# The kv, query and gate products of a sparse-attention layer: fp32 products against three split fp32r products

## The reference, cut to what matters

```python
def rmsnorm(x, g):
    return x * rsqrt(mean(x * x, -1) + EPS) * g

u  = rmsnorm(h, kv_norm)              # D = 1024
kv = (u @ kv_w)                       # 1024 x 1536: k_c v_c | k_s v_s k_w v_w (4 groups x 64 each)
k_s, k_w = rope(rmsnorm(k_s, ..)), rope(rmsnorm(k_w, ..))
k_cmp, v_cmp = compress(k_c, ..), compress(v_c, ..)   # 15 blocks of 32 tokens, two small matmuls, gelu
z  = rmsnorm(h, b_norm) @ b_w_in      # 1024 x (1024 queries + 48 gates)
q  = rope(rmsnorm(z[:, :1024]))       # 16 heads x 64
gates = sigmoid(z[:, 1024:] + gate_b)
o  = gates_0 * attend(q, k_cmp, v_cmp) + gates_1 * attend(q, k_s, v_s) + gates_2 * attend(q, k_w, v_w)
h  = h + o @ b_w_out
```

## Time and profile before

| | |
|---|---|
| median of 3 runs | 2376.24 us (2375.14 to 2376.44) |
| profiled execution | 2374.76 us, of which span 2373.1 us |
| busy in the span | PE 97%, DVE 72%, ACT 58%, POOL 4% |
| granted TensorE clock | mean 0.993 of full speed |
| end of ffn0 to the first `scores` | 297.43 to 408.27 us |
| attention steps | 408.27 to about 478 us |

### The profile page before, as it was taken

One profiled execution on the slowest core, in us unless ns is written; L12 is line 12 of the kernel. 1 busy time (PEld: TensorE's weight loads), 2 busy tenths in 40 slices (PEclk: granted clock), 3 DMA queues, 4 the chain that ended last, 5 costly groups with the idle time before them and its releaser, 6 DMA issues.

```text
span 2373.1 us, 31549 instructions
## 1 busy us (share of the span) xinstructions
PE 2307.4 (97%) x12242; PEld 1936.0 (82%) x12242; DVE 1698.0 (72%) x1609; ACT 1373.7 (58%) x1217; POOL 100.4 (4%) x111
## 2 busy tenths in 40 slices
PE   7999999999999999999999989999999999999998
PEld 6878845888889878888899788888888888888886
DVE  6655544755457676555567769898989888888897
ACT  4633312644336865334467557777777777777775
POOL 0000020000000110000011001000000000000020
PEclk9999999999999999999999999999999999999999
DMA  6455354055435335554353389999999999999993
GB/s 231 168 211 212 142 213 164 1 185 195 167 136 178 107 133 195 205 212 180 113 178 107 108 316 414 395 381 377 390 368 384 374 390 369 389 370 389 369 382 125
DMA packets 204633, 588.63 MB, mean 248 GB/s; under 512 B 9164, under 2 KB 17552, under 8 KB 204544
## 3 DMA queue, kind: packets, MB, share of 16 engines
q1 hardware_dynamic: 197696, 564.28, 63.8%
q0 software_dynamic: 6656, 23.04, 2.6%
q10 hardware_dynamic: 192, 0.05, 0.0%
HBM read 573.19 MB, written 14.16 MB: 247 GB/s over the span
## 4 chain that ended last, share of the span: by engine, by line
PE 94%; DVE 3%; ACT 1%; issue 1%; DMA 1%; ACTq 0%; DVEq 0%
PE ps L1386 9%; PE ps L1385 9%; PE ps L1387 9%; PE ps L781 8%; PE ps L783 8%; PE ps L782 8%; PE ps L666 4%; PE ps L1425 4%; PE ps L1424 4%; PE ps L1426 4%; PE ps L676 3%; PE ps L675 3%; PE ps L677 3%; PE ps L658 2%; PE ps L1159 1%; PE ps L1160 1%
## 5 line engine op out<-in xcount | busy, mean ns | idle before, releaser
L2038 DVE TENSOR_TENSOR more_low<-more_parts,high_parts 128x2048 fp32r<-128x2048 f32 x192 | 431.9, 2287 | 35.8 <-ACT high_parts L1494 34.7
L1494 ACT ACTIVATE high_parts<-more_parts 128x2048 fp32r<-128x2048 f32 x192 | 364.4, 1918 | 101.4 <-PE ps L1426 51.8
L1385 PE MATMUL ps<-high_parts,xmh 128*128 128x512 f32 x896 | 352.5, 393 | 2.4 <-issue 2.4
L1387 PE MATMUL ps<-high_parts,xml 128*128 128x512 f32 x896 | 349.1, 390 | 0.0
L2038 DVE TENSOR_TENSOR raw_low<-raw,high_parts 128x2048 fp32r<-128x2048 f32 x144 | 323.9, 2286 | 27.9 <-ACT high_parts L1494 27.9
L1494 ACT ACTIVATE high_parts<-raw 128x2048 fp32r<-128x2048 f32 x144 | 275.8, 1920 | 93.1 <-PE ps L1387 49.8
L1609 ACT ACTIVATE wh<-raw 128x4096 fp32r<-128x4096 f32 (+1 forms) x57 | 196.6, 3451 | 190.6 <-PE ps L783 179.8
L2209 DVE TENSOR_TENSOR wl<-raw,wh 128x4096 fp32r<-128x4096 f32 (+1 forms) x57 | 239.2, 4197 | 60.5 <-ACT wh L1609 60.5
L781 PE MATMUL ps<-wh,xh 128*128 128x512 f32 (+1 forms) x632 | 244.0, 386 | 3.4 <-issue 2.8
L783 PE MATMUL ps<-wh,xl 128*128 128x512 f32 (+1 forms) x632 | 239.6, 379 | 0.0
L782 PE MATMUL ps<-wl,xh 128*128 128x512 f32 (+1 forms) x632 | 239.5, 379 | 0.0
(11 more groups left out here) (545 smaller groups left out, 4441.7 us busy)
## 6 DMA issues: line engine op xcount, KB each, us to landing
more_parts<-in_moe_w_gate SPq DMA_DIRECT2D x78, 1024.0 KB, 5.1
more_parts<-in_moe_w_up SPq DMA_DIRECT2D x66, 1024.0 KB, 7.0
raw<-in_moe_w_down SPq DMA_DIRECT2D x64, 1024.0 KB, 6.4
more_parts<-in_moe_w_down SPq DMA_DIRECT2D x48, 1024.0 KB, 5.7
raw<-in_moe_w_up SPq DMA_DIRECT2D x46, 1024.0 KB, 5.3
raw<-in_w_in SPq DMA_DIRECT2D x22, 2048.0 KB, 8.0
raw<-in_f_w_in SPq DMA_DIRECT2D x20, 2048.0 KB, 8.6
raw<-in_moe_w_gate SPq DMA_DIRECT2D x34, 1024.0 KB, 6.8
```

Of the source, the lines that this page charges most:

```text
L1385: mm(o, xmh[:, k, :], hi[:, cs], start=(k == 0), stop=False)
L1387: t = mm(o, xml[:, k, :], hi[:, cs], start=False, stop=(k == KD - 1))
L1494: fn(part_high(j), part_raw(j), ACT.Copy).then_inc(hi_done, 1)
L2038: v.tensor_tensor(part_low(j), part_raw(j), part_high(j).bitcast(F32), ALU.subtract).then_inc(lo_done, 1)
```

## The change

The plain fp32 products of kv, queries and gates become split products. `uh` holds the high part of the transposed hidden state and `ul` the low part, without a norm weight. The norm weight goes into the weight tile: ACT writes high halves (`high_k`: weight times gain, as fp32r) and DVE low halves (`low_k`: weight times gain minus high). A half is 4 of the 8 steps `k` of one weight tile, 128 x 2048 elements; the list `K_HALVES` has eleven, with the buffer of the high part of each (`bh`, `wmh[:, 0]`, `wmh[:, 1]`, once `wmo[:, 0]`), and `k_free` says when a buffer's former reader is done.

```diff
+        K_HALVES = [(("kv", 0), "kv_norm", range(0, 4), 512, bh), (("kv", 0), "kv_norm", range(4, 8), 512, wmh[:, 1]),
+                    (("b_in", 0), "b_norm", range(0, 4), 512, wmh[:, 0]), (("b_in", 0), "b_norm", range(4, 8), 512, bh),
+                    (("b_in", 1), "b_norm", range(0, 4), 512, wmh[:, 1]), (("b_in", 1), "b_norm", range(4, 8), 512, wmh[:, 0]),
+                    (("b_in", 2), "b_norm", range(0, 8), 3 * NH, bh),
+                    (("kv", 1), "kv_norm", range(0, 4), 512, wmh[:, 1]), (("kv", 1), "kv_norm", range(4, 8), 512, wmh[:, 0]),
+                    (("kv", 2), "kv_norm", range(0, 4), 512, bh), (("kv", 2), "kv_norm", range(4, 8), 512, wmo[:, 0])]
# PE
+            def k_product(b, i, m, c0=0, n=None):
...
+                for k in ks:
+                    o, cs = ps[:, b, 0:n], slice(c0, c0 + n)
+                    mm(o, uh[:, k, ms], hi[:, k - ks[0], cs], start=(k == 0), stop=False)
+                    mm(o, uh[:, k, ms], lo[:, k, cs], start=False, stop=False)
+                    t = mm(o, ul[:, k, ms], hi[:, k - ks[0], cs], start=False, stop=(k == KD - 1))
...
+            queries_of(0)
+            queries_of(1)
 
             pe.wait_ge(kvc_in, 16 * 2 * 2 * NG)
...
-            product(me.a, ("b_in", 1), 1, ubT)
...
+            halves_split()
             for m in range(M):
-                product(me.v, ("b_in", 2), m, ubT, w=3 * NH)
+                k_product(me.v.claim(pe), 6, m).then_inc(v_filled, 1)
...
+            halves_split(2)
+            window_part(me.v, 0, 0)
             me.see(kc_ready)
...
+            window_part(me.a, 1, 0)
...
+            turn_keys(0)
+            window_part(me.v, 0, 256)
             turn_keys(1)
+            window_part(me.a, 1, 256)
+            released(("kv", 2), me.a)
# ACT
+            def high_k(i):
...
+                for k in ks:
+                    t = fn(hi[:, k - ks[0], :], src[:, k, :], ACT.Copy, scale=col(gain, k))
+                t.then_inc(mh_ready, 1)
# DVE
+            def low_k(i):
...
+                for k in ks:
+                    t = v.scalar_tensor_tensor(dst[:, k, :], src[:, k, :], col(gain, k), hi[:, k - ks[0], :].bitcast(F32),
+                                               ALU.mult, ALU.subtract)
+                t.then_inc(ml_ready, 1)
...
+            low_k(7)
+            low_k(8)
+            low_k(9)
+            low_k(10)
             keys_values(1)
# POOL
             po.wait_ge(zeroed_set, 1)
+            po.wait_ge(exp_done, 2)
```

More of the change, by code:

```diff
@@ L976, in _ @@
             turned_hidden = me.a.n
-            product(me.a, ("kv", 1), 1, uT)
-            released(("kv", 1), me.a)
+            halves_split(2)
+            b = me.v.claim(pe)
+            k_product(b, 7, 0)
+            k_product(b, 8, 0).then_inc(v_filled, 1)
             pe.wait_ge(a_read, turned_hidden)
@@ L1670, in ffn @@
                 body(nb - 1, FB, FB, last=True)
+                if ahead:
+                    ahead()
                 high_h_last(FFN_END[name] - 1)
-            ffn(0)
+            def high_k(i):
+                key, gain, ks, w, _ = K_HALVES[i]
+                arrived(act, key)
+                hi, src = k_high(i), tile_view(key, KD, w)
+                for k in ks:
+                    t = fn(hi[:, k - ks[0], :], src[:, k, :], ACT.Copy, scale=col(gain, k))
+                t.then_inc(mh_ready, 1)
+            ffn(0, ahead=lambda: high_k(0))
+            act.wait_ge(u_done, FFN_END["ffn0"])
+            high_k(1)
+            for m in range(M):
+                for j in range(2):
+                    b = me.s.take(act)
+                    fn(uh[:, 4 * j:4 * j + 4, m * P:(m + 1) * P], ps[:, b, :].rearrange("p (k t) -> p k t", k=4),
+                       ACT.Copy).then_inc(norm_h, 1)
+                squares(m)
+            square_root()
+            high_k(2)
             fn(ident_r[:], C("ident"), ACT.Copy).then_inc(causal_ready, 1)
             fn(causal_r[:], C("neg_causal"), ACT.Copy).then_inc(causal_ready, 1)
[L1678 to L1686, removed]
+            act.wait_ge(*k_free[0])
+            high_k(3)
             def root(n, rows=P):
@@ L1717, in _ @@
             root(NH // 2)
+            root(NH // 2)
+            act.wait_ge(*k_free[5])
+            high_k(7)
+            high_k(8)
             me.see(gate_ready)
@@ L1736, in _ @@
             t.then_inc(a_read, 1)
+            act.wait_ge(*k_free[6])
+            high_k(9)
+            high_k(10)
             root(NG)
+            root(NG, NCMP)
             keys_values(1)
             root(NG)
-            root(NG, NCMP)
+            root(NG)
+            b = me.a.take(act)
+            fn(kvn[:, 1, 768:1024], ps[:, b, 0:256], ACT.Copy, scale=small[:, 7:8]).then_inc(a_read, 1)
+            marks["keys", 2] = me.a.n
+            root(NG)
             turned_keys(0)
-            root(NG)
-            keys_values(2)
-            root(NG)
             turned_keys(1)
@@ L1747, in _ @@
             fn(cs[:], cs[:], ACT.Exp, scale=SCALE).then_inc(cexp_ready, 1)
+            b = me.a.take(act)
+            fn(vv[:, 1, 1, :, 0:HD], ps[:, b, 0:256].rearrange("p (g d) -> p g d", g=NG), ACT.Copy,
+               scale=small[:, 7:8]).then_inc(a_read, 1)
             def probs(i):
@@ L2294, in ffn, with low_turned @@
                 dve.nop().then_inc(d_added, 1)
[L2296 to L2306, removed]
+            def low_k(i):
+                key, gain, ks, w, _ = K_HALVES[i]
+                me.see(mh_ready)
+                hi, src, dst = k_high(i), tile_view(key, KD, w), tile_view(key, KD, w, raw_low)
+                for k in ks:
+                    t = v.scalar_tensor_tensor(dst[:, k, :], src[:, k, :], col(gain, k), hi[:, k - ks[0], :].bitcast(F32),
+                                               ALU.mult, ALU.subtract)
+                t.then_inc(ml_ready, 1)
+            def low_turned():
+                for j in range(2):
+                    b = me.s.take(dve)
+                    me.see(norm_h)
+                    ks, ms = slice(4 * j, 4 * j + 4), slice(me.low_m * P, (me.low_m + 1) * P)
+                    v.tensor_tensor(ul[:, ks, ms], ps[:, b, :].rearrange("p (k t) -> p k t", k=4), uh[:, ks, ms].bitcast(F32),
+                                    ALU.subtract).then_inc(s_read, 1)
+                me.low_m += 1
+            me.low_m = 0
+            ffn(0, beside=low_turned, ahead=lambda: low_k(0))
+            low_k(1)
+            low_turned()
             mean_squares()
+            low_k(2)
             b = me.v.take(dve)
@@ L2408, in _ @@
             t.then_inc(v_read, 1)
-            keys_values(2)
-            key_phase(1, 0)
+            key_phase(0, 1)
+            dve.nop().then_inc(k_ready, 1)
+            b = me.v.take(dve)
+            v.tensor_scalar(kvn[:, 0, 768:1024], ps[:, b, 0:256], small[:, 6:7], None, ALU.mult).then_inc(v_read, 1)
+            dve.wait_ge(v_read, me.v.n)
             b = me.v.take(dve)
```

97 lines of the change are left out of this document (66 added, 31 removed).

## The result

| | before | after |
|---|---|---|
| median | 2376.19 us (2375.02 to 2376.44, 8 runs) | 2383.80 us (2381.95 to 2384.74, 8 runs) |
| ratio to before | | 1.0030, 95% interval 1.0021 to 1.0040 |
| span of the profiled execution | 2373.1 us | 2382.7 us |
| granted TensorE clock, mean | 0.993 | 0.985 |

The page of after stands against the earlier trace rows: PE has no less busy time, but 4.3 us more (0.4 in after_again), although ten fp32 products have become split ones, and less of the last chain is PE's.

The account below looks back on a forecast made before the run. PE, busy 97% of the span, was taken as the bound. Scores 4.3 us earlier plus 1.1 from the clock, say 5.5, gave 2374.76 - 5.5 = 2369.3, plus 1.5 to the median's scale: 2370.7 us; range 2364 to 2380.

Parts of the forecast that it names:

- The step that failed: PE behind the xcT wait: transposes and gates until 346.0, then the compress product in 14.0 us, ending at 360.0.
- a gain of 1.1 at the scores: PE before the attention: last window parts, keys and scores at full rate, so the scores' 2.9 us shrink by 1.1.
- the forecast of the stage (5.4 less): Stage up to the attention: scores start 4.3 us earlier and run 1.1 us shorter, sum 5.4, say 5.5.
- the clock stays low: Rival, chance 0.10: half rate from the wait before 384 holds until the scores; gain about 1, so 2375 us.
- Split steps: PE's split products: three matmuls of 512 columns take 0.68 us, so eight k take 5.45 us instead of 6.9.
- Halves: Making weight halves: a high one 2.1 us on ACT, a low one 2.5 us on DVE, upper bound 3.0.
- Loads of kv: Weight loads for the compress product: kv 1 lands 8.5 us after release, kv 2 from 360.0 to 367.8.
- the weights come late: Rival, chance 0.16: kv 2 lands in 16.0 us instead of 7.8, a loss of 5.5, so 2381.7 us.
- Zeros in the attention: The write of zeros moves from 325 us into the attention, where queues are idle; cost 0.
- PE's 14.4 us less to do: PE's own work in the stage could shrink by 14.4 us; not taken as the gain, since halves must be made.
- The rule against it: Stage's head: POOL's fill of zeroed and DVE's low halves with two SBUF inputs contend, one waiting for the other.
- that rival (0.18): DVE held by the fill, chance 0.18: DVE waits 3.6 us, gain 2.4 to 0, about 2374.5 us.

Follow-up runs that it names:

- after_again: The changed kernel, unchanged, measured a second time: 2381.17 us, ratio 1.0016 to before.
- a7: Changed kernel with 48 gate matmuls dealt out among 24 wide ones, xc transposes behind them, gates and xcT ahead of the last two query norms on DVE: 2368.88 us.
- a5: Changed kernel with the low steps of kv 2 done a second time on DVE into a scratch tile: 2389.6 us, ratio 1.0057.
- b3: Kernel before with only the write of zeros moved to wait for the attention's second exp: 2376.11 us, ratio 0.9997.
- b2: Kernel before with the zeros' write late and DVE's xcT additions ahead of the last query norm: 2369.6 us, ratio 0.9973.
- a1: Changed kernel with 24 wide matmuls, result unused, on PE in its wait for xcT: 2377.86 us, ratio 1.0004.
- a2: Changed kernel with the gates' product ahead of the xc transposes on PE and the gate operations ahead of the xcT additions on DVE: 2372.21 us, ratio 0.9982.
- a4: Changed kernel with b_in 1 multiplied by tokens, xc transposes ahead of its last half, xcT ahead of the norms: 2372.64 us, ratio 0.9986.
- b1: Kernel before with DVE's xcT additions ahead of the last query norm: 2376.4 us, ratio 0.9995.
- a9: a4 with only high x high in the gates, 16 narrow matmuls instead of 48: 2370.63 us, ratio 0.9972.

## Why the prediction was wrong

Times of after are set back by 2.3 us here, by which its stage started later than before's.

**The step that failed** is the sentence "Four transposes and 48 gate matmuls, the first 20 or so at half rate, take it to 346.0; the compress product starts there ... and takes 14.0". I took the length of the half clock from before, 5 us after PE went on the earlier trace rows. But there a wide fp32 product followed the wait; the change had moved the gates to that place. All 48 ran at half rate, transposes and gates took 11.1 us instead of 8.3, and the compress product 16.5. With the `xcT` wait ending at 338.8 and not 337.7, the product ended at 366.3, 6.3 us later than forecast. Of these 6.3, 1.1 are DVE's halves ahead of `xcT` and 5.2 are the clock, low for longer than forecast. From there the error is handed on: kv 2 landed at 374.4 (forecast 367.8), low ended at 382.3 (375.0), `kc_ready` fell at 391.3 (384.2), `kcb` at 398.1 (390.9). a7 shows it the other way round: without the low clock the compress product took 14.02.

**Then the clock once more.** I had full rate for the last window parts, keys and scores, a gain of 1.1 at the scores. In after the clock came back at about 398.2 and fell again at about 401.6, in the 32 narrow matmuls of L1062; it stayed low until 411.9. The turned keys and the window part behind them took 6.4 us instead of 3.8 (406.19 to 412.55). The scores themselves did have full rate: 1.5 us from their start to the first maximum, 2.6 in before. Of the 10 us between the forecast of the stage (5.4 less) and the result (4.6 more), 7.2 stood at `kcb` and 2.8 came here; in all 8.0 are the clock. The rival "the clock stays low", with 0.10, had the second fall and not the first, and so 2375.

**Terms that held or nearly.** Split steps of 0.227 us. Halves: low 2.74 us (forecast 2.5), high 2.56 (forecast 2.1, from copies out of PSUM); 0.2 to 0.5 each, and a5 shows that on kv 2 they put off the keys in full. That makes up the 1.1 at `xcT` and 0.7 of the landing-to-keys row. Loads of kv: 8.5 and 7.9 us (forecast 8.5 and 7.8), so "the weights come late" was wrong, and that its 2381.7 is the nearest number is luck. Zeros in the attention: 0 (b3; from the first maximum to the output product 67.8 us in both kernels). PE's 14.4 us less to do were never collected: a7's stage is 10.3 us shorter than before's, and 7.9 of that the fp32 kernel has too in b2.

**The rule against it.** POOL's timeline beside DVE's, at the stage's head:

```profile
300.19 3.65 POOL L3243 MEMSET zeroed<- 128x4216 f32 x1
```

```profile
299.11 2.73 DVE L2390 SCALAR_TENSOR_TENSOR raw_low<-raw,cols,wmh 128x512 fp32r<-128x512 f32 x4
```

Neither is longer than elsewhere: 3.63 us in the earlier trace rows, 2.74 for the other halves. This fill did not collide with these two-input DVE steps, and that rival (0.18) is out. The Trainium skill (GPSIMD Engine Reference, Specifications) speaks of contention with DVE instructions that have two SBUF inputs; no run here shows it for a fill.

**The range** of 2364 to 2380 was too narrow at its upper end because each rival carried one fault; the two clock terms and the halves came together.

**Why slower and not merely level.** The first low clock used up what the split products had saved (both kernels end the compress product at 366.3). The loss of 4.6 us then came behind it: kv 2 lands and needs 7.9 us of high and low halves before DVE can start its keys, PE waits 7.0 us, and the clock falls twice more. a1 moves the first part and a5 the second, each alone.

## What to carry to other kernels

When a change moves work behind a wait, ask what kind of work it is: in this stage, in all sixteen executions, a low clock came back while PE did matmuls of 128 to 512 columns and never in those of 30 or 48, so narrow work there is charged double and hands the low clock on to what follows. Where it can be done, deal narrow matmuls out among wide ones, as a7 did. Give the old kernel the same care before the new one is credited: b2's two edits brought most of what a7 has. And before a wait is costed, look for a second one that ends at the same place: here taking away either alone gave nothing.

## What the runs showed of the hardware

- The granted clock fell to half while PE was never idle: in a2 the gates began at 330.75 with PE busy since 298, and from 334 on the clock was 0.50. 48 fp32r matmuls of 48 columns in a row did it in a1, a2 and a4; 48 dealt out among 24 wide ones did not (a7). The 32 fp32 records of the same product, 3.7 us in a row behind a wide one, did not in b1, but 32 fp32 ones of 30 columns (L1010) did in b2, at their end. Where the border lies between them is not shown.
- A wait of 2.10 us left the clock at 1.00 in a4; one of 2.19 us in a9 was followed by a fall, 0.7 us after PE went on. The one of 5.40 us took it down in before, 3.6 us after PE fell idle.
- In after the waits of 1.34 and 5.41 us, with the narrow work behind them, left PE at half clock for some 20 us (337 to 357). It came back 5.1 us after wide work began, as in before (5.0).
- A high half of 4 x (128 x 512) from SBUF to fp32r took 2.56 us on ACT, where copies from PSUM took 2.06.
